# Opening of a two-layer fp32 kernel: the eight modulation weight units get memory of their own (that of the rounded weights), TensorE takes two of their products, GpSimd none, VectorE six, and the first unit starts on half of the features

## Chip, cores and metric

The kernel runs on one core of a Trainium2 chip. The metric is the device time of one execution in microseconds (us), as the median of three executions; beside it stands one profiled execution, from which all rows are read.

## The reference, cut to what matters

Two transformer-like blocks follow each other on 256 tokens of 1024 features. The change touches only the beginning of the first one:

```
c_act = silu(c)                                   # 1024 values
mod   = c_act @ w_mod + b_mod                     # 1024 x 3072; shift, scale, gate
h     = rms_norm(x, g_norm) * (1 + scale) + shift
proj  = h @ w_in                                  # 1024 x 8192, the first big product
```

`shift` and `scale` need two thirds of `w_mod`: 1024 rows of 2048 numbers, 8 MB. Everything after `proj` (a gated linear recurrence, dilated attention, output products, and then the second block with four feed-forward networks) depends on `h`.

## The kernel before, in words

All weights of the program lie in device memory as a row of "units" of 128 partitions x 2048 fp32 (1 MB each). SyncE's queue (SP) loads them in order into `raw`, a ring of four slots (`RING`). Each unit u that is a matmul weight is split in two: ScalarE writes its rounded part `whi` (`hi()`, L380) and VectorE the rest `wlo = raw - whi` (`lo()`, L1096); TensorE multiplies each with `feed_hi` and `feed_lo`, the two parts of the activations, in three passes (L1860 to L1862). One unit is 12 matmuls of 512 columns for each of the two token tiles t = 0, 1. A group is four units; TensorE does all four for t = 0, then for t = 1.

The first eight units, r = 0 to 7, are the modulation weights: unit r holds 128 rows of `w_mod`, one row on each partition. The sum over rows is made in two steps: an engine multiplies the unit by the column `c_act[:, r]` (one number for each partition), and TensorE then adds up the partitions by 16 matmuls with one column of ones (L1983, result in `aux`). Before the change GpSimd makes the products of r = 0 and 3 (`MOD_POOL`, L1033), VectorE adds up those of the other six in `mod_part` (L1246, the last one in two halves, L1251). The units use the same four slots of `raw` as all others, so the load of unit r + 4 waits until the product of unit r has been made (`wait_mod`), and the first matmul units u = 0 to 3 wait for those of r = 4 to 7.

Every engine has a program of its own, written out in order; semaphores tie them together. VectorE's order in the opening is: the sine and cosine tables (L1205 to L1233), the normalized rows `xn` (L1238), its modulation products, `lo(2)` for units 0 and 1, the sum of `aux` parts into `mod` and `scale_g` (L1256 to L1262), then for each token tile eight times `full = turn * scale_g + mod` (L1270, a chunk of 128 features each, from the transposed rows in `turn`), twice `feed_lo = full - feed_hi` (L1282), and `lo()` for the next unit. ScalarE makes `hi` of units 0 to 2, then `feed_hi` (L454) in halves of four chunks. TensorE waits at its first unit until both halves of `feed_lo` are there:

```
if g == 0:
    pe.wait_ge(first_fed, 2 * t + 2)
```

Its transposes of the rows of t = 1 stand ahead of that unit in its program. The second four of them need the second half of `turn` free, which is so when the last of the eight L1270 has run.

Of the kernel before, what the change touches and what calls it, by code (L numbers as in the profile page):

```python
# [70 lines left out]


# [8 lines left out]
MOD_POOL = (0, 3)  # L81
# [24 lines left out]
def build(nc, io):  # L106
    with ExitStack() as ctx:
# [8 lines left out]
        def sb(name, shape, dtype=F32):  # L116
# [8 lines left out]
        wlo = sb("wlo", [P, RING, UNIT], F32R)  # L125
        h = sb("h", [P, TOK, D])
# [62 lines left out]
        mod_pool = [placed("mod_pool0", [P, 2 * D], F32, base[0]),  # L189
                    placed("mod_pool1", [P, 2 * D], F32, base[0] - 4 * HEADS * SEQ)]  # L190
# [85 lines left out]
        setup_loaded = sem("setup_loaded")  # L276
        x_loaded = sem("x_loaded")
# [10 lines left out]
        mod_pooled = sem("mod_pooled")  # L288
# [58 lines left out]
        def mod_count(r):  # L347

            return sum((k in MOD_POOL) == (r in MOD_POOL) for k in range(r + 1))

        def wait_mod(engine, r):
            engine.wait_ge(mod_pooled if r in MOD_POOL else mod_used, mod_count(r))

# [12 lines left out]
        def _(act):  # L366
            n = {"u": 0, "e": [0, 0], "first": 0, "used": 0, "tb": 0, "ss": 0, "h": 0, "ple": 0, "mix": 0, "pre": 0}

            def hi(times=1, it=None):

                for _ in range(times):
# [5 lines left out]
                    act.wait_ge(loaded[u % RING], more * 16 + 16 * (raw_of(u) // RING + 1))  # L377
                    if u >= RING:
                        act.wait_ge(unit_used, more * RING + (u - RING + 1))
# [556 lines left out]
        def _(sp):  # L936
            sp.dma_start(cols[:, :], io["cols"]).then_inc(setup_loaded, 16)
            sp.dma_start(pos_i[:, :], io["pos_cols"]).then_inc(setup_loaded, 16)
            sp.dma_start(invf[:, :], io["invf"].partition_broadcast(P)).then_inc(setup_loaded, 16)
            sp.dma_start(h[:, :, :], io["x"].rearrange("(t p) d -> p t d", p=P)).then_inc(x_loaded, 16)  # L940
            sp.dma_start(ident[:, :], io["ident"]).then_inc(x_loaded, 16)
            for r in range(N_MOD1):
                if r >= RING:
                    wait_mod(sp, r - RING)
                sp.dma_start(raw[:, r % RING, :], io["units"][r]).then_inc(loaded[r % RING], 16)
            for j in range(RING):
                wait_mod(sp, N_MOD1 - RING + j)
                sp.dma_start(raw[:, j, :], io["units"][N_MOD1 + j]).then_inc(loaded[j], 16)
# [34 lines left out]
        def _(pool):  # L983
# [91 lines left out]
        def _(dve):  # L1075
# [118 lines left out]
            mark(dve.memset(mod_part[:, :], 0.0))  # L1194
            dve.wait_ge(setup_loaded, 16 * 3)
# [8 lines left out]

            mark(dve.tensor_copy(pos_f[:, :], pos_i[:, :]))  # L1205
# [35 lines left out]
            for r in range(N_MOD1):  # L1241
                if r in MOD_POOL:
                    continue
                dve.wait_ge(loaded[r % RING], 16 * (r // RING + 1))
                if r < N_MOD1 - 1:
                    dve.scalar_tensor_tensor(mod_part[:, :], raw[:, r % RING, :], c_act[:, r:r + 1], mod_part[:, :],  # L1246
                                             ALU.mult, ALU.add).then_inc(mod_used, 1)
# [1251 lines left out]
```

## Time and profile before

| what | value |
|---|---|
| median of three executions | 1509.49 us (1508.46 to 1510.73) |
| profiled execution, its own time | 1509.22 us |
| its span, first to last instruction | 1507.4 us |
| TensorE busy | 1435.8 us, 95% |
| VectorE busy | 886.2 us, 59% |
| ScalarE busy | 709.0 us, 47% |
| GpSimd busy | 100.8 us, 7% |
| loads | 272.52 MB, mean 181 GB/s |

The profiled execution's time is 1.8 us over its span (what lies around the span) and 0.3 us under the median. The opening is the stretch from 0 to about 53 us, where the first big matmul starts.

### The profile page before, as it was taken

Reading aid. Unit: us, or ns where it says so; the run is one execution under the profiler, and the core shown is the slowest. Engines: PE = TensorE matmul, PEld = TensorE weight load, DVE = VectorE, ACT = ScalarE, POOL = GpSimd, SP = SyncE. Lnnn points to the kernel's source line nnn. Section 1 sums busy time; section 2 is a strip of 40 time slices with the busy share of each in tenths; the row PEclk is TensorE's granted clock in tenths of the full one; section 3 lists DMA queues with packets and bytes.
Section 4 is the critical chain, followed back from the end, with each engine's and each line's share of the span. In section 5 each row is a group of like instructions: output and inputs, shape, how many; then the busy total and the mean of one; then the engine's idle time right before and its main releaser. Section 6 shows DMA issues by size and latency. Waiting matters only on the chain.

```text
span 1507.4 us, 17138 instructions
## 1 busy us (share of the span) xinstructions
PE 1435.8 (95%) x6622; PEld 1184.3 (79%) x6622; DVE 886.2 (59%) x818; ACT 709.0 (47%) x701; POOL 100.8 (7%) x95
## 2 busy tenths in 40 slices
PE   4899899899999999999999999999999999999997
PEld 4788777677888877788888877888888877888886
DVE  8856575976555465656545375554676354744535
ACT  2446756445454355745434354453544453543433
POOL 3000100002000020011000010000101110200001
PEclk9999999999999999999999999999999999999999
DMA  6754433574645544336445465645455454645541
GB/s 258 305 204 178 156 114 112 192 278 160 223 171 194 195 166 155 113 138 209 155 179 198 164 227 192 223 161 201 164 199 194 149 178 150 227 150 194 184 179 42
DMA packets 40510, 272.52 MB, mean 181 GB/s; under 512 B 4866, under 2 KB 5890, under 8 KB 8835
## 3 DMA queue, kind: packets, MB, share of 16 engines
q1 hardware_dynamic: 36992, 261.65, 48.0%
q10 hardware_dynamic: 3458, 10.04, 1.9%
q8 instruction: 43, 0.70, 0.2%
q14 instruction: 17, 0.13, 0.0%
HBM read 270.62 MB, written 1.05 MB: 180 GB/s over the span
## 4 chain that ended last, share of the span: by engine, by line
PE 83%; DVE 11%; ACT 3%; issue 2%; DMA 1%; POOL 0%; DVEq 0%; SPq 0%; POOLq 0%; ACTq 0%
PE acc L1860 25%; PE acc L1862 25%; PE acc L1861 25%; PE turn L1913 3%; DVE wlo L1096 3%; ACT whi L380 1%; DMA raw<-in_units 1%; DVE gate_part L1484 1%; PE aux L2164 1%; DVE xn L1150 1%; DVE h L1166 1%; DVE red L1227 1%; DVE feed_lo L1134 0%; PE turn L2014 0%; PE aux L2320 0%
## 5 line engine op out<-in xcount | busy, mean ns | idle before, releaser
L1096 DVE TENSOR_TENSOR wlo<-raw,whi 128x2048 fp32r<-128x2048 f32 x233 | 533.4, 2300 | 276.7 <-ACT whi L380 276.6
L1860 PE MATMUL acc<-whi,feed_hi 128*128 128x512 f32 (+1 forms) x1504 | 601.0, 400 | 11.7 <-DVE feed_lo L1134 7.8
L1862 PE MATMUL acc<-whi,feed_lo 128*128 128x512 f32 (+1 forms) x1504 | 588.6, 391 | 0.0
L1861 PE MATMUL acc<-wlo,feed_hi 128*128 128x512 f32 (+1 forms) x1504 | 587.8, 391 | 0.0
L380 ACT ACTIVATE whi<-raw 128x2048 fp32r<-128x2048 f32 x233 | 445.6, 1916 | 291.9 <-PE acc L1862 264.4
L1860 PEld LDWEIGHTS acc<-whi,feed_hi 128*128 128x128 f32 x1504 | 285.1, 190 | 71.3 <-issue 10.5
L1862 PEld LDWEIGHTS acc<-whi,feed_lo 128*128 128x128 f32 x1504 | 284.9, 189 | 60.7
L1861 PEld LDWEIGHTS acc<-wlo,feed_hi 128*128 128x128 f32 x1504 | 285.5, 190 | 56.8 <-issue 1.2
L1860 PE MATMUL acc<-whi,hid_hi 128*128 128x512 f32 x352 | 138.0, 392 | 0.0
L1862 PE MATMUL acc<-whi,hid_lo 128*128 128x512 f32 x352 | 137.1, 389 | 0.0
L1861 PE MATMUL acc<-wlo,hid_hi 128*128 128x512 f32 x352 | 137.0, 389 | 0.0
L1862 PEld LDWEIGHTS acc<-whi,hid_lo 128*128 128x128 f32 x352 | 66.1, 188 | 13.8
L1861 PEld LDWEIGHTS acc<-wlo,hid_hi 128*128 128x128 f32 x352 | 66.1, 188 | 13.3
L1860 PEld LDWEIGHTS acc<-whi,hid_hi 128*128 128x128 f32 x352 | 66.1, 188 | 13.3
L608 ACT ACTIVATE hid_hi<-turn 128x512 f32 (+2 forms) x48 | 26.4, 550 | 99.2 <-PE turn L1913 99.2
L1513 DVE TENSOR_TENSOR hid_lo<-turn,hid_hi 128x512 f32 (+2 forms) x48 | 30.8, 642 | 71.7 <-ACT hid_hi L608 71.7
L997 POOL TENSOR_SCALAR ms<-ss 128x1 f32<-128x1 f32 x20 | 14.7, 733 | 863.8 <-ACT xn L400 823.8
L1913 PE MATMUL turn<-ident,xn 128*128 128x128 f32 x250 | 36.4, 286 | 32.6 <-DVE xn L1238 20.5
L1913 PEld LDWEIGHTS turn<-ident,xn 128*128 128x128 f32 x250 | 30.3, 147 | 38.8 <-issue 23.6
L1504 DVE SCALAR_TENSOR_TENSOR hid<-acc,pre_rs,sgl 128x512 f32<-128x512 f32 (+1 forms) x48 | 33.8, 704 | 44.9 <-ACT sgl L601 41.0
L1134 DVE TENSOR_TENSOR feed_lo<-turn,feed_hi 128x512 fp32r<-128x512 f32 x48 | 31.0, 685 | 35.1 <-ACT feed_hi L422 35.1
L422 ACT ACTIVATE feed_hi<-turn 128x512 fp32r<-128x512 f32 x48 | 26.1, 592 | 49.3 <-PE turn L1913 49.0
(312 smaller groups left out, 898.7 us busy)
## 6 DMA issues: line engine op xcount, KB each, us to landing
raw<-in_units SPq DMA_DIRECT2D x245, 1024.0 KB, 4.9
gpost<-in_norm_g ACTq DMA_DIRECT2D x8, 512.0 KB, 5.0
gpre<-in_norm_g ACTq DMA_DIRECT2D x6, 512.0 KB, 6.3
h<-in_x SPq DMA_DIRECT2D x1, 1024.0 KB, 5.9
w_ax<-in_w_ax SPq DMA_DIRECT2D x1, 1024.0 KB, 9.4
bgate<-in_b_gate SPq DMA_DIRECT2D x1, 1024.0 KB, 12.0
out<-h SPq DMA_DIRECT2D x2, 512.0 KB, 2.6
decay<-in_decay ACTq DMA_DIRECT2D x1, 768.0 KB, 4.5
```

Source lines behind the costliest of these rows:

```text
L380: act.activation(whi[:, u % RING, :], raw[:, u % RING, :], ACT.Copy).then_inc(hi_ready, 1)
L422: act.activation(dst[:, 4 * i:4 * i + 4, lanes(t)], turn[:, b, :].rearrange("p (c s) -> p c s", c=4), ACT.Copy).then_inc(fed_hi, 1)
L608: act.activation(dst, turn[:, b, 0:P * count].rearrange("p (c s) -> p c s", c=count), ACT.Copy).then_inc(fed_hi, 1)
L1096: dve.tensor_tensor(wlo[:, u % RING, :], raw[:, u % RING, :], whi[:, u % RING, :].bitcast(F32), ALU.subtract).then_inc(lo_ready, 1)
L1134: dve.tensor_tensor(dst[part], turn[:, b, :].rearrange("p (c s) -> p c s", c=4), hi_part[part].bitcast(F32), ALU.subtract).then_inc(moved[ ...
L1150: dve.tensor_tensor(xn[:, t, halves[half]], h[:, t, halves[half]], gpre[:, halves[half]], ALU.mult)\
L1504: dve.scalar_tensor_tensor(hid[:, t, 0:tiles, :], up, pre_rs[:, t:t + 1], sgl[:, t, 0:tiles, :], ALU.mult, ALU.mult)\
L1513: dve.tensor_tensor(hid_lo[:, at, lanes(t)], turn[:, b, 0:P * count].rearrange("p (c s) -> p c s", c=count), hid_hi[:, at, lanes(t)].bitca ...
L1860: pe.matmul(out, xh, wh, start=first, stop=False)
L1861: pe.matmul(out, xh, wl, start=False, stop=False)
L1862: return pe.matmul(out, xl, wh, start=False, stop=last)
L1913: last = pe.transpose(turn[:, b, P * i:P * i + P], part, ident[:, :])
```

## The change

What it does: `mod_raw`, 8 units of room, is laid over `whi` and `wlo` (4 + 4 slots), which nothing uses before unit 0. Modulation unit r lands in it, each with a semaphore of its own, and the first four matmul units land in `raw`; none of these twelve loads waits. Instead, ScalarE waits before it writes `whi[u]` (that is where unit r = u lay) until the product of r = u is made; `wlo[j]` lies over unit r = 4 + j, which VectorE itself has read. TensorE makes the products of r = 0 and 1 itself: 16 matmuls each with the unit as weights and `c_act[:, r]` as the moving column. GpSimd has none. VectorE makes r = 2 to 7, the first as a plain product, so the clearing of `mod_part` goes. VectorE adds TensorE's two parts and the bias before `lo(2)`, and the third after it. The small loads of positions, `invf` and `ident` go from SP's queue to the start of ScalarE's queue, and the waits are split (`cols`, the two table inputs, `x`, `ident`). The work of a token tile on VectorE is interleaved, and TensorE's unit 0 waits for the first half of `feed_lo` alone, unit 1 for the second.

```
+        mod_raw = placed("mod_raw", [P, N_MOD1, UNIT], F32, base[0] - 8 * RING * UNIT)
...
         def wait_mod(engine, r):
-            engine.wait_ge(mod_pooled if r in MOD_POOL else mod_used, mod_count(r))
+            if r in MOD_PE:
+                engine.wait_ge(mod_columns, MOD_PE.index(r) + 1)
+            else:
+                engine.wait_ge(mod_used, mod_count(r))
...  ScalarE, hi()
-                    if u >= RING:
+                    if u < RING:
+                        wait_mod(act, u)
+                    else:
                         act.wait_ge(unit_used, more * RING + (u - RING + 1))
...  ScalarE, start
-            act.wait_ge(setup_loaded, 16 * 3)
+            act.dma_start(pos_i[:, :], io["pos_cols"]).then_inc(setup_loaded, 16)
+            act.dma_start(invf[:, :], io["invf"].partition_broadcast(P)).then_inc(setup_loaded, 16)
+            act.dma_start(ident[:, :], io["ident"]).then_inc(ident_loaded, 16)
+            act.wait_ge(cols_loaded, 16)
             act.activation(c_act[:, :], cols[:, COL["c"]:COL["c"] + KC], ACT.Silu).then_inc(c_ready, 1)
-            act.wait_ge(x_loaded, 16 * 2)
+            act.wait_ge(x_loaded, 16)
...  SyncE
-            sp.dma_start(cols[:, :], io["cols"]).then_inc(setup_loaded, 16)
-            sp.dma_start(pos_i[:, :], io["pos_cols"]).then_inc(setup_loaded, 16)
-            sp.dma_start(invf[:, :], io["invf"].partition_broadcast(P)).then_inc(setup_loaded, 16)
+            sp.dma_start(cols[:, :], io["cols"]).then_inc(cols_loaded, 16)
             sp.dma_start(h[:, :, :], io["x"].rearrange("(t p) d -> p t d", p=P)).then_inc(x_loaded, 16)
-            sp.dma_start(ident[:, :], io["ident"]).then_inc(x_loaded, 16)
             for r in range(N_MOD1):
-                if r >= RING:
-                    wait_mod(sp, r - RING)
-                sp.dma_start(raw[:, r % RING, :], io["units"][r]).then_inc(loaded[r % RING], 16)
+                sp.dma_start(mod_raw[:, r, :], io["units"][r]).then_inc(mod_loaded[r], 16)
             for j in range(RING):
-                wait_mod(sp, N_MOD1 - RING + j)
                 sp.dma_start(raw[:, j, :], io["units"][N_MOD1 + j]).then_inc(loaded[j], 16)
...  GpSimd
-            pool.wait_ge(c_ready, 1)
-            for r, product in zip(MOD_POOL, mod_pool):
-                pool.wait_ge(loaded[r % RING], 16 * (r // RING + 1))
-                pool.tensor_scalar(product[:, :], raw[:, r % RING, :], c_act[:, r:r + 1], None, ALU.mult)\
-                    .then_inc(mod_pooled, 1)
...  VectorE
-            mark(dve.memset(mod_part[:, :], 0.0))
-            dve.wait_ge(setup_loaded, 16 * 3)
+            dve.wait_ge(cols_loaded, 16)
...
+            dve.wait_ge(setup_loaded, 16 * 2)
             mark(dve.tensor_copy(pos_f[:, :], pos_i[:, :]))
...
+            dve.wait_ge(mod_columns, len(MOD_PE))
             mark(dve.tensor_tensor(mod[:, :], aux[:, 0, 0:2 * KC], cols[:, COL["b_mod"]:COL["b_mod"] + 2 * KC], ALU.add))
             settle()
+            mark(dve.tensor_tensor(mod[:, :], aux[:, 0, 2 * KC:4 * KC], mod[:, :], ALU.add))
+            settle()
+            dve.wait_ge(mods_ready, 1)
+            dve.wait_ge(mod_used, mod_count(N_MOD1 - 1))
+            lo(2)
+
+            dve.wait_ge(mod_summed, 1)
+            mark(dve.tensor_tensor(mod[:, :], aux[:, 1, 0:2 * KC], mod[:, :], ALU.add))
...
             for t in range(TOK):
+                modulated(t, next_turn(), 0, range(4))
+                b = next_turn()
+                modulated(t, b, 1, range(2))
+                first_rest(t, 0)
+                modulated(t, b, 1, range(2, 4))
+                first_rest(t, 1)
                 lo()
...  TensorE
+            for i, r in enumerate(MOD_PE):
+                pe.wait_ge(mod_loaded[r], 16)
                 for f in range(2 * KC):
                     at = 2 * KC * i + f
-                    last = pe.matmul(aux[:, 0, at:at + 1], part[:, P * f:P * f + P], ones[:, 0:1],
+                    last = pe.matmul(aux[:, 0, at:at + 1], mod_raw[:, r, P * f:P * f + P], c_act[:, r:r + 1],
                                      start=True, stop=True)
+                last.then_inc(mod_columns, 1)
+                if i == 0:
+                    feed_rows(xn[:, 0, :], staged_dve, "dve")
...
-                    if g == 0:
-                        pe.wait_ge(first_fed, 2 * t + 2)
+                if g == 0 and i < 2:
+                    pe.wait_ge(first_fed, 2 * t + i + 1)
```

`modulated(t, b, i, part)` is the old loop over L1270 for some of the chunks of half i, and `first_rest(t, i)` the old L1282 with its wait for `feed_hi`.

SyncE's queue, from the start of the program. Before:

```order
1 L937 DMA cols<-in_cols 128x104
2 L938 DMA pos_i<-in_pos_cols 128x4
3 L939 DMA invf<-in_invf 128x176
4 L940 DMA h<-in_x 128x2x1024
5 L941 DMA ident<-in_ident 128x128
6 L945 DMA raw<-in_units 128x2048 x4
7 L945 DMA raw<-in_units 128x2048 [waits mod_pooled]
8 L945 DMA raw<-in_units 128x2048 [waits mod_used] x2
9 L945 DMA raw<-in_units 128x2048 [waits mod_pooled]
10 L948 DMA raw<-in_units 128x2048 [waits mod_used] x4
11 L949 DMA w_ax<-in_w_ax 128x2048
```

and of the change:

```order
1 L951 DMA cols<-in_cols 128x104
2 L952 DMA h<-in_x 128x2x1024
3 L954 DMA mod_raw<-in_units 128x2048 x8
4 L956 DMA raw<-in_units 128x2048 x4
5 L957 DMA w_ax<-in_w_ax 128x2048
6 L958 DMA bias_124<-in_bias 128x384
```

Eight waits are gone from between the loads, and three small loads have left this queue.

VectorE, from the end of `lo(2)` (the two `wlo`) to the first `lo()` behind it. Before:

```order
30 L1096 TENSOR_TENSOR wlo<-raw,whi 128x2048 [waits hi_ready] x2
31 L1256 TENSOR_TENSOR mod<-aux,cols 128x16 [waits mod_summed]
32 L1260 TENSOR_TENSOR mod<-aux,mod 128x16 [waits dve_step] x2
33 L1262 SCALAR_TENSOR_TENSOR scale_g<-mod,cols 128x8 [waits dve_step]
34 L1270 TENSOR_SCALAR full<-turn,scale_g,mod 128x128 [waits turned0,dve_step]
35 L1270 TENSOR_SCALAR full<-turn,scale_g,mod 128x128 x2
36 L1270 TENSOR_SCALAR full<-turn,scale_g,mod 128x128 [waits dve_step]
37 L1270 TENSOR_SCALAR full<-turn,scale_g,mod 128x128 [waits turned1]
38 L1270 TENSOR_SCALAR full<-turn,scale_g,mod 128x128 x2
39 L1270 TENSOR_SCALAR full<-turn,scale_g,mod 128x128 [waits dve_step]
40 L1282 TENSOR_TENSOR feed_lo<-full,feed_hi 128x4x128 [waits fed_hi] x2
41 L1096 TENSOR_TENSOR wlo<-raw,whi 128x2048 [waits hi_ready]
```

and of the change:

```order
33 L1268 TENSOR_TENSOR mod<-aux,mod 128x16 [waits mod_summed]
34 L1270 SCALAR_TENSOR_TENSOR scale_g<-mod,cols 128x8 [waits dve_step]
35 L1277 TENSOR_SCALAR full<-turn,scale_g,mod 128x128 [waits turned0,dve_step]
36 L1277 TENSOR_SCALAR full<-turn,scale_g,mod 128x128 x2
37 L1277 TENSOR_SCALAR full<-turn,scale_g,mod 128x128 [waits dve_step]
38 L1277 TENSOR_SCALAR full<-turn,scale_g,mod 128x128 [waits turned1]
39 L1277 TENSOR_SCALAR full<-turn,scale_g,mod 128x128
40 L1290 TENSOR_TENSOR feed_lo<-full,feed_hi 128x4x128 [waits fed_hi]
41 L1277 TENSOR_SCALAR full<-turn,scale_g,mod 128x128
42 L1277 TENSOR_SCALAR full<-turn,scale_g,mod 128x128 [waits dve_step]
43 L1290 TENSOR_TENSOR feed_lo<-full,feed_hi 128x4x128 [waits fed_hi]
44 L1099 TENSOR_TENSOR wlo<-raw,whi 128x2048 [waits hi_ready]
```

Two small sums have moved ahead of the two `wlo`, and the first `feed_lo` stands between the sixth and the seventh chunk instead of behind the eighth. On TensorE, as it is now, the transposes of t = 1 still stand ahead of unit 0:

```order
10 L2004 MATMUL aux<-ones,mod_part 128x1 x7
11 L1929 MATMUL turn<-ident,xn 128x128 [waits moved0,staged_dve]
12 L1929 MATMUL turn<-ident,xn 128x128 x3
13 L1929 MATMUL turn<-ident,xn 128x128 [waits moved1]
14 L1929 MATMUL turn<-ident,xn 128x128 x3
15 L1876 MATMUL acc<-whi,feed_hi 128x512 [waits lo_ready,first_fed]
```

Here only the wait of the last row has changed its count; `moved1` is raised by the eighth chunk.

## Rows read from the trace of the kernel before

**Rows 1.** Busy time by stretch: stretch, length, PE, PEld, DVE, ACT, POOL, clock, DMA share, GB/s

```profile
60.00:120.00 60.00, 60.00 (x283) 49.94 (x282) 33.32 (x53) 27.71 (x21) 0.00 (x0) 1.00 0.47 171
```

**Rows 2.** Waits of TensorE, 0 to 110 us: total, times, longest

```profile
PE turn L1913 <- DVE xn L1238: 20.5, 1, 20.5
```

**Rows 3.** Timeline to 26 us (start, length, what); the first row is of the chain

```profile
1.65 4.79 DMA invf<-in_invf
...
9.17 1.65 DVE L1227 SCALAR_TENSOR_TENSOR red<-trn,red 128x352 f32<-128x352 f32 x3
...
12.54 5.04 DVE L1227 SCALAR_TENSOR_TENSOR red<-trn,red 128x352 f32<-128x352 f32 x3
13.48 5.46 POOL L1033 TENSOR_SCALAR mod_pool<-raw,c_act 128x2048 f32<-128x2048 f32 x1
...
17.62 1.51 DVE L1231 TENSOR_SCALAR red<-red 128x352 f32<-128x352 f32 x1
...
19.56 0.74 DVE L1238 TENSOR_SCALAR xn<-h,rs 128x1024 f32<-128x1024 f32 x1
...
19.75 5.86 POOL L1033 TENSOR_SCALAR mod_pool<-raw,c_act 128x2048 f32<-128x2048 f32 x1 [0.81 <-DMA raw<-in_units]
...
20.22 5.93 DVE L1238 TENSOR_SCALAR xn<-h,rs 128x1024 f32<-128x1024 f32 x1
```

**Rows 4.** Timeline, 33 to 48.3 us

```profile
33.39 2.35 DVE L1246 SCALAR_TENSOR_TENSOR mod_part<-raw,c_act,mod_part 128x2048 f32<-128x2048 f32 x1 [0.21 <-DMA raw<-in_units]
...
38.45 2.48 DVE L1251 SCALAR_TENSOR_TENSOR mod_part<-raw,c_act,mod_part 128x1024 f32<-128x1024 f32 x2
...
39.78 6.98 PE L1983 MATMUL aux<-ones,mod_part 128*128 128x1 f32 x32 [3.95 <-DVE mod_part L1251]
...
43.32 1.91 ACT L380 ACTIVATE whi<-raw 128x2048 fp32r<-128x2048 f32 x1 [0.56 <-DMA raw<-in_units]
45.26 2.29 DVE L1096 TENSOR_TENSOR wlo<-raw,whi 128x2048 fp32r<-128x2048 f32 x1 [0.18 <-ACT whi L380]
...
47.31 1.91 ACT L380 ACTIVATE whi<-raw 128x2048 fp32r<-128x2048 f32 x1 [2.08 <-DMA raw<-in_units]
...
48.09 0.17 DVE L1262 SCALAR_TENSOR_TENSOR scale_g<-mod,cols 128x8 f32<-128x8 f32 x1
```

**Rows 5.** Loads: the one issued at 3.10, then two of one stretch

```profile
raw<-in_units SPq DMA_DIRECT2D x1, 1024.0 KB, 9.2
...
L945 SPq DMA_DIRECT2D raw<-in_units x2: 635/672/710, 4.2 to 5.0; - x2
...
DMA to landing us min/median/max: 13.0/13.9/14.7
```

**Rows 6.** Timeline, 48.3 to 62 us

```profile
48.29 2.90 DVE L1270 TENSOR_SCALAR full<-turn,scale_g,mod 128x128 f32<-128x128 f32 x8
49.89 0.63 ACT L454 ACTIVATE feed_hi<-full 128x512 fp32r<-128x512 f32 x1 [0.66 <-DVE full L1270]
...
51.25 1.11 PE L1913 MATMUL turn<-ident,xn 128*128 128x128 f32 x4 [0.23 <-DVE full L1270]
...
51.95 0.69 DVE L1282 TENSOR_TENSOR feed_lo<-full,feed_hi 128x512 fp32r<-128x512 f32 x1 [0.16 <-ACT feed_hi L454]
52.56 2.29 DVE L1096 TENSOR_TENSOR wlo<-raw,whi 128x2048 fp32r<-128x2048 f32 x1
...
52.70 0.79 PE L1860 MATMUL acc<-whi,feed_hi 128*128 128x512 f32 x1 [0.33 <-DVE feed_lo L1282]
...
59.02 2.29 DVE L1096 TENSOR_TENSOR wlo<-raw,whi 128x2048 fp32r<-128x2048 f32 x1
...
61.91 0.39 PE L1860 MATMUL acc<-whi,feed_hi 128*128 128x512 f32 x1
```

**Rows 7.** Loads by line over the whole span: count, KB, median us to landing

```profile
gpre<-in_norm_g ACTq DMA_DIRECT2D x6, 512.0 KB, 6.3
...
ident<-in_ident SPq DMA_DIRECT2D x1, 64.0 KB, 7.2
```

More of the change, by code:

```diff
@@ L287, in build @@
         mod_used = sem("mod_used")
-        mod_pooled = sem("mod_pooled")
+        mod_loaded = [sem(f"mod_loaded{r}") for r in range(N_MOD1)]
+        mod_columns = sem("mod_columns")
         mods_ready = sem("mods_ready")
@@ L347, in mod_count @@
         def mod_count(r):
-            return sum((k in MOD_POOL) == (r in MOD_POOL) for k in range(r + 1))
+            return sum(k not in MOD_PE for k in range(r + 1))
         def wait_mod(engine, r):
-            engine.wait_ge(mod_pooled if r in MOD_POOL else mod_used, mod_count(r))
+            if r in MOD_PE:
+                engine.wait_ge(mod_columns, MOD_PE.index(r) + 1)
+            else:
+                engine.wait_ge(mod_used, mod_count(r))
         def chunks(ap, n=4):
@@ L376, in hi @@
                     more = 0 if it is None else it
-                    act.wait_ge(loaded[u % RING], more * 16 + 16 * (raw_of(u) // RING + 1))
-                    if u >= RING:
+                    act.wait_ge(loaded[u % RING], more * 16 + 16 * (loads_of(u) // RING + 1))
+                    if u < RING:
+                        wait_mod(act, u)
+                    else:
                         act.wait_ge(unit_used, more * RING + (u - RING + 1))
@@ L1240, in _ @@
             dve.wait_ge(c_ready, 1)
[L1241 to L1246, printed above, removed]
+            for r in range(len(MOD_PE), N_MOD1):
+                dve.wait_ge(mod_loaded[r], 16)
+                if r == len(MOD_PE):
+                    dve.tensor_scalar(mod_part[:, :], mod_raw[:, r, :], c_act[:, r:r + 1], None, ALU.mult)\
+                        .then_inc(mod_used, 1)
+                elif r < N_MOD1 - 1:
+                    dve.scalar_tensor_tensor(mod_part[:, :], mod_raw[:, r, :], c_act[:, r:r + 1], mod_part[:, :],
@@ L1257, in _ @@
             settle()
-            for i in range(len(MOD_POOL)):
-                at = 2 * KC * (i + 1)
-                mark(dve.tensor_tensor(mod[:, :], aux[:, 0, at:at + 2 * KC], mod[:, :], ALU.add))
-                settle()
             mark(dve.scalar_tensor_tensor(scale_g[:, :], mod[:, KC:2 * KC], 1.0,
@@ L1968, in group_deep @@
                         hooks[2]()
-            pe.wait_ge(x_loaded, 16 * 2)
-            feed_rows(xn[:, 0, :], staged_dve, "dve")
+            pe.wait_ge(ident_loaded, 16)
             pe.wait_ge(pads_ready, 1)
-            for i, part in enumerate(mod_pool + [mod_part]):
-                if part is not mod_part:
-                    pe.wait_ge(mod_pooled, i + 1)
+            pe.wait_ge(c_ready, 1)
+            for i, r in enumerate(MOD_PE):
+                pe.wait_ge(mod_loaded[r], 16)
                 for f in range(2 * KC):
-                    if part is mod_part and f == 0:
-                        pe.wait_ge(mods_ready, 1)
-                    if part is mod_part and f == KC:
-                        pe.wait_ge(mod_used, mod_count(N_MOD1 - 1))
                     at = 2 * KC * i + f
-                    last = pe.matmul(aux[:, 0, at:at + 1], part[:, P * f:P * f + P], ones[:, 0:1],
+                    last = pe.matmul(aux[:, 0, at:at + 1], mod_raw[:, r, P * f:P * f + P], c_act[:, r:r + 1],
                                      start=True, stop=True)
+                last.then_inc(mod_columns, 1)
+                if i == 0:
+                    feed_rows(xn[:, 0, :], staged_dve, "dve")
+            for f in range(2 * KC):
+                if f == 0:
+                    pe.wait_ge(mods_ready, 1)
+                if f == KC:
+                    pe.wait_ge(mod_used, mod_count(N_MOD1 - 1))
+                last = pe.matmul(aux[:, 1, f:f + 1], mod_part[:, P * f:P * f + P], ones[:, 0:1], start=True, stop=True)
             last.then_inc(mod_summed, 1)
```

52 lines of the change are left out of this document (27 added, 25 removed).

## Prediction

> **What bounds the kernel now.** I read the busy time by stretch first. Behind the opening TensorE is busy for 60.00 of 60 us [rows 1]; there the other engines only have to keep up. TensorE's longest wait is 20.5 us for the first normalized rows [rows 2], and its first big matmul starts at 52.70 [rows 6]. So the change can move one number, the start of that matmul; what it moves is moved for the whole program, as all later waits are relative to TensorE.
>
> The chain of waits up to 52.70, from its end: `feed_lo` (51.95 + 0.69) released the matmul; before it stand the eight L1270 from 48.29 [rows 6], `scale_g` at 48.09, ready at 48.26, and ahead of that the `wlo` of unit 1, which began at 45.26 behind ScalarE's `whi` at 43.32, which waited for the landing of unit 1 [rows 4]. TensorE's last pass over `mod_part` (39.78 + 6.98 = 46.76) was done earlier. Unit 1 landed late because each load waited for a ring slot, that is for products, and these were late because VectorE was. GpSimd's products ran 13.48 to 18.94 and 19.75 to 25.61. VectorE's three L1227 took 5.04 us beside the first of them and 1.65 without it, L1231 took 1.51 where I put 0.36 (an estimate: `xn`, nearly three times as long, takes 0.74), `xn` took 5.93 beside the second and 0.74 ahead of it [rows 3]. That is 3.4 + 1.15 + 5.2 = 9.7 us of VectorE's time lost beside GpSimd.
>
> **The loads.** Units r = 0, 2 and 3 were issued at 3.10, 4.2 and 5.0 and landed after 9.2, 13.0 and 14.7 us, at 12.3, 17.2 and 19.7 [rows 5]: 2.5 us each. r = 5 landed at 33.3 and unit 1, four later, at 43.3 [rows 4]: 2.5 again. Unit 2 then came at 47.3, 4.0 us later, a slip of 1.5 us. Now twelve loads stand in the queue without a wait. `h` is issued two places earlier, by 0.93 us at SP's pace; since the bytes of `invf` and `ident` still pass through the same engines, I take 0.5 us. So r = 3 lands at 19.2, r = 7 at 29.2, unit 0 at 31.7, unit 1 at 34.2, unit 2 at 36.7. Bounds: 1.5 us earlier (r = 0 is issued 1.45 us earlier) and 1.5 us later (one slip).
>
> **Path by the loads.** From unit 1's landing to `scale_g` ready it took 48.26 - 43.32 = 4.94 us [rows 4]. Two of the small sums, 0.2 us each, are now done before, so 4.54: 34.2 + 4.54 = 38.7. I call this moment M; before it was 48.26.
>
> **Path by the products.** VectorE's last product in two halves takes 2.48, its first half 1.28; r = 7 landed at 29.2, with 0.2 for the wait and 1.28 TensorE can start at 30.7. Its 32 rows take 6.98 [rows 4], 37.7; with 0.1 for the signal and 0.4 for the sum and `scale_g` M would be 38.2. This path loses by 0.5. TensorE is free for it: 6.98 for r = 0 from 11.8 gives 18.8, 1.9 for the transposes (L1913, eight of them; four took 1.11 [rows 6]) 20.7, r = 1 27.7. That cost is hidden by the wait for VectorE; the cover is 3.0 us.
>
> **Path by the tables.** `invf` landed at 1.65 + 4.79 = 6.44, and `xn` was ready at 26.15; less 9.7 that is 16.4, or landing + 10.0 [rows 3]. A plain product of 2048 is not in the trace; between 0.74 (half the size, [rows 3]) and 2.35 (the sum with product, [rows 4]) I take 1.35, since the same kind of instruction at half the size takes 0.74. Then four of 2.35, 1.28, TensorE's 6.98 and 0.7 for the waits and small sums: M = landing of `invf` + 29.7, so 36.2 at 6.44. It stays hidden as long as `invf` lands before 9.0. Clearing `mod_part` lay in the wait for the loads and is worth nothing.
>
> **From M to the matmul.** Before: 52.70 - 48.26 = 4.44. Now: four chunks of 0.36 (2.90 for eight) end at M + 1.5, ScalarE's `feed_hi` runs M + 1.6 to 2.3 [rows 6], VectorE does two chunks meanwhile, `feed_lo` M + 2.3 to 3.0, the last two chunks to M + 3.8. The half start would allow the matmul at M + 3.1. But TensorE's second four transposes stand ahead of it and wait for the eighth chunk, which is now behind `feed_lo`: they start at M + 3.85 and hold TensorE some 0.9 of their 1.11 us. So the first matmul starts at M + 4.8, 0.35 later than before. The edit that is named for a start on half of the features gives nothing by itself: by the order of rows it costs 0.35.
>
> It also delays VectorE. The second `feed_lo` now waits for `feed_hi` of the eighth chunk with nothing to do meanwhile: M + 3.9 to 4.55 on ScalarE, `feed_lo` to M + 5.3, against M + 4.4 before. `wlo` of unit 2 (2.29) ends at M + 7.5, and it is wanted at M + 11.3. Then t = 1, which took 59.02 - 52.56 = 6.46 from `wlo` to `wlo` [rows 6], takes the same 0.6 more: `wlo` of unit 3 starts at M + 12.35 and ends at M + 14.65. TensorE reaches unit 3 after 61.91 - 52.70 = 9.2 [rows 6], at M + 14.0. There it waits 0.65. Before, that unit was ready at 61.31 for 61.91. Behind it VectorE has slack and the rest follows TensorE.
>
> ScalarE makes `whi` of unit 2 before `feed_hi`: landing 36.7 + 1.91 = 38.6, wanted at M + 1.6 = 40.3; with the slip of 1.5 it is 40.1, just hidden.
>
> **Sum.** Matmul at 38.7 + 4.8 = 43.5 instead of 52.70, 9.2 earlier; less 0.65 at unit 3: 8.55 us. The profiled execution took 1509.22, which is 0.27 under the median: 1509.22 - 8.55 = 1500.7 us.
>
> **A rule that bears on it.** In the trace loads of ScalarE's queue land after 6.3 us in the middle (`gpre`), beside SP's units; `ident`, on SP's queue behind `h`, took 7.2 [rows 7]. Issued at about 1.2, `invf` would land at 7.5 by the first, before 9.0, and cost nothing; at 8.4 by the second, again nothing. The Trainium skill, "DMA: Bandwidth & Descriptors", section on queues, rings and completion order, says that each DMA engine goes round the queues that have work and changes only after a whole packet. By that rule `invf` would wait behind one packet of `h` or of a unit, not behind the whole stream; the sum would be the one above. The trace has no small load beside twelve waiting ones, so this stays a rival.
>
> **The rivals.**
> The loads come sooner (0.2): unit 1 at 32.7, r = 7 at 27.7. Then the products' path gives M = 36.7 and the loads' path 37.2; the matmul comes at 42.0, the saving is 10.05: 1499.2. For it: the stream starts earlier and is never interrupted. Against it: 2.5 us per unit was the same in both stretches.
>
> `invf` is late on ScalarE's queue (0.2): at 12 us M = 41.7, the saving 5.55, 1503.7. For it: it shares the engines with `h` and megabytes behind it from its first moment, where it had them nearly alone before. Against it: the 6.3 us of `gpre`.
>
> A slip in the stream hits unit 1 (0.08), as it hit unit 2: M = 40.2, 1502.2; with two slips 1503.7.
>
> Slower (0.03): ScalarE's queue is served only after SP's stream, so that `invf` lands behind the units. VectorE's chain is then the opening. It decides from a landing at 17.5 us on: M = 47.2, and with the 0.35 + 0.65 above the saving is nil. After ten units (26.7) it would be M = 56.4 and 1518.4. Against it: `gpre` lands in the middle of a stream of units.
>
> The change doesn't do what it says (0.02): `invf` at 14.5 to 17.5, or TensorE waiting elsewhere later for what it no longer waits for here, gives 1506.5 to 1509. Against it: TensorE's 60.00 of 60 us [rows 1] behind the opening.
>
> **How the numbers follow.** My forecast's own case has 0.47, with 1499.7 to 1501.8 for the bounds of the hand-over (0.35 and 0.65 both gone, or 1 us more if the first 36 matmuls, which stood 0.256 us apart [rows 6], stand 0.03 farther apart). The range reaches from the early case less its hand-over terms, 1498.0, to the late `invf` and slips, 1504.5. A measurement of this kernel tells about 0.2%, 3.0 us, from no change: faster takes the first four cases, 0.95; no change 0.02; slower 0.03.
>
> **What would show it.** Right: the first L1876 at 43.5, not 52.70; a wait of 0.4 to 0.9 us of TensorE for `wlo` at unit 3; its wait for `xn` down to nothing beyond 18.8, since r = 0 fills it; `whi` of unit 1 waiting for its load at about 34; VectorE's `xn` ready by 17.5. Wrong: `invf` later than 9 us, L1230 (the old L1227) still in the tables at 18, TensorE's products of r = 1 ending past 30.7, or the ten loads farther apart than 2.5 us.

## The result and the profile after

| | median | range |
|---|---|---|
| before | 1510.11 us (4 executions) | 1508.46 to 1512.11 |
| changed | 1500.46 us (4 executions) | 1498.02 to 1501.50 |

The ratio is 0.9932, 95% interval 0.9916 to 0.9949: 9.65 us faster by the medians, 7.7 to 12.7 by the interval. Predicted were 1500.7 us. The profiled execution of the changed kernel took 1498.02 us, with a span of 1496.0.

The timeline of the changed kernel's opening (start, length, engine, what; in brackets the idle time before it and what ended it):

```profile
10.12 1.64 DVE L1230 SCALAR_TENSOR_TENSOR red<-trn,red 128x352 f32<-128x352 f32 x3
...
11.31 6.98 PE L1994 MATMUL aux<-c_act,mod_raw 128*128 128x1 f32 x32 [11.31 <-DMA ident<-in_ident]
...
13.49 1.64 DVE L1230 SCALAR_TENSOR_TENSOR red<-trn,red 128x352 f32<-128x352 f32 x3
...
16.59 0.75 DVE L1241 TENSOR_SCALAR xn<-h,rs 128x1024 f32<-128x1024 f32 x1
...
17.25 1.28 DVE L1247 TENSOR_SCALAR mod_part<-mod_raw,c_act 128x2048 f32<-128x2048 f32 x1
...
28.59 2.48 DVE L1254 SCALAR_TENSOR_TENSOR mod_part<-mod_raw,c_act,mod_part 128x1024 f32<-128x1024 f32 x2
...
29.93 6.99 PE L2004 MATMUL aux<-ones,mod_part 128*128 128x1 f32 x32 [3.21 <-DVE mod_part L1254]
...
33.50 1.91 ACT L391 ACTIVATE whi<-raw 128x2048 fp32r<-128x2048 f32 x1 [0.58 <-DMA raw<-in_units]
...
37.21 1.91 ACT L391 ACTIVATE whi<-raw 128x2048 fp32r<-128x2048 f32 x1 [1.79 <-DMA raw<-in_units]
...
37.86 0.17 DVE L1270 SCALAR_TENSOR_TENSOR scale_g<-mod,cols 128x8 f32<-128x8 f32 x1
...
40.31 0.69 DVE L1290 TENSOR_TENSOR feed_lo<-full,feed_hi 128x512 fp32r<-128x512 f32 x1
...
41.83 1.11 PE L1929 MATMUL turn<-ident,xn 128*128 128x128 f32 x4 [1.04 <-DVE full L1277]
...
42.53 0.69 DVE L1290 TENSOR_TENSOR feed_lo<-full,feed_hi 128x512 fp32r<-128x512 f32 x1 [0.76 <-ACT feed_hi L468]
42.59 0.77 PE L1876 MATMUL acc<-whi,feed_hi 128*128 128x512 f32 x1
...
50.41 2.28 DVE L1099 TENSOR_TENSOR wlo<-raw,whi 128x2048 fp32r<-128x2048 f32 x1
```

Both series of three L1230 take 1.64 us, and the second `xn` 0.75, where [rows 3] had 5.04 and 5.93. The load of unit 1 lands at 33.50 and not at 43.32 [rows 4]; `scale_g` is ready at M = 38.03, the first big matmul starts at 42.59. The same stretch shows the two things that were forecast against the change: the first half of `feed_lo` is ready at 41.00, but the transposes ahead of the matmul wait 1.04 us for the eighth chunk, and the second `feed_lo` stands behind 0.76 us of idle time.

The waits of TensorE from 40 us on (engine, line, waited for: total, times, longest), and the chain where it comes to unit 3:

```profile
PE turn L1929 <- DVE full L1277: 3.8, 2, 2.8
PE acc L1876 <- DVE wlo L1099: 0.2, 1, 0.2
...
50.50 2.21 DVE wlo L1099
52.75 0.50 PE acc L1876
```

Here M is, as in the prediction, the moment when `scale_g` is ready. `wlo` of unit 3 ends at 52.69, M + 14.66, and TensorE starts unit 3 at 52.75. Before it was 61.91 [rows 6]. Up to here the change has brought 9.16 us between these two profiles. The span is 11.4 us shorter; the other 2.2 lie behind unit 3, where a second profile of the changed kernel (below) does not show them.

Why the wait is 0.2 and not the forecast 0.65 is seen in the starts of the first matmuls of unit 0:

```profile
45.30 0.63 PE L1876 MATMUL acc<-whi,feed_hi 128*128 128x512 f32 x1
45.73 0.52 PE L1877 MATMUL acc<-wlo,feed_hi 128*128 128x512 f32 x1
46.08 0.39 PE L1878 MATMUL acc<-whi,feed_lo 128*128 128x512 f32 x1
46.31 0.39 PE L1876 MATMUL acc<-whi,feed_hi 128*128 128x512 f32 x1
```

They start 0.43 us apart up to 45.73, and 0.23 apart from 46.08 on. 512 columns in 0.43 us are 1.2 GHz; the shorter step fits the 2.4 GHz level better than the lower one (my inference from the steps: the granted-clock column reads 1.00 for the whole opening all the same). The kernel before:

```profile
54.14 0.63 PE L1860 MATMUL acc<-whi,feed_hi 128*128 128x512 f32 x1
54.57 0.47 PE L1861 MATMUL acc<-wlo,feed_hi 128*128 128x512 f32 x1
54.87 0.40 PE L1862 MATMUL acc<-whi,feed_lo 128*128 128x512 f32 x1
55.11 0.39 PE L1860 MATMUL acc<-whi,feed_hi 128*128 128x512 f32 x1
```

It had the short step from 54.87 on, 2.2 us after its first matmul; here that came 3.5 us after. So TensorE came to unit 3 later by 0.6 us and found `wlo` nearly ready. I call the time from the first matmul to the first short step the slow stretch.

This bears on the 9.16 too. Before the change TensorE did not wait at unit 3 (`wlo` was ready at 61.31), so 61.91 moves with the slow stretch. With one of 3.5 us it would have been some 62.5, and the change would have brought some 9.8 (an estimate from these rows).

### The profile page after: what moved, and what is told of

It reads as the page before. It is cut to its first block, busy times and chain, and to the rows that moved or that the text cites. A ratio compares the mean times of both kernels' runs of the same rounds, so it can differ in the third digit from the quotient of the medians.

```text
span 1496.0 us, 17141 instructions
## 1 busy us (share of the span) xinstructions
PE 1433.3 (96%) x6622; PEld 1182.6 (79%) x6622; DVE 873.4 (58%) x817; ACT 709.1 (47%) x701; POOL 89.9 (6%) x93
## 3 DMA queue, kind: packets, MB, share of 16 engines
HBM read 270.62 MB, written 1.05 MB: 182 GB/s over the span
## 4 chain that ended last, share of the span: by engine, by line
PE 82%; DVE 10%; ACT 3%; issue 2%; DMA 2%; SPq 0%; POOL 0%; DVEq 0%; POOLq 0%; ACTq 0%
PE acc L1876 25%; PE acc L1878 25%; PE acc L1877 25%; PE turn L1929 3%; DVE wlo L1099 3%; DMA raw<-in_units 2%; ACT whi L391 1%; DVE gate_part L1500 1%; PE aux L2184 1%; DVE xn L1153 1%; DVE h L1169 1%; DVE feed_lo L1137 0%; PE turn L2034 0%; PE aux L2340 0%; PE aux L2215 0%
## 5 line engine op out<-in xcount | busy, mean ns | idle before, releaser
L1876 PE MATMUL acc<-whi,feed_hi 128*128 128x512 f32 (+1 forms) x1504 | 600.3, 399 | 11.4 <-DVE feed_lo L1137 7.9
L1878 PEld LDWEIGHTS acc<-whi,hid_lo 128*128 128x128 f32 x352 | 66.1, 188 | 13.8
L1929 PE MATMUL turn<-ident,xn 128*128 128x128 f32 x250 | 37.4, 291 | 12.2 <-DVE xn L1153 8.3
```

What stands on the lines that cost most here:

```text
L1876: pe.matmul(out, xh, wh, start=first, stop=False)
L1878: return pe.matmul(out, xl, wh, start=False, stop=last)
L1929: last = pe.transpose(turn[:, b, P * i:P * i + P], part, ident[:, :])
```

## The experiments

"Unit 3" is the start of its first matmul at t = 0, the 37th big matmul (idle-time ones not counted); whatever waits in the opening lies ahead of it. A line that begins with "..." has all edits of the lines above it, from "transposes behind unit 0" on. All are read from one profiled execution each.

| kernel | M | first matmul | unit 3 | span less unit 3 | granted clock |
|---|---|---|---|---|---|
| before | 48.26 | 52.70 | 61.91 | 1445.5 | 0.990 |
| changed | 38.03 | 42.59 | 52.75 | 1443.3 | 0.992 |
| changed, again | 38.11 | 42.68 | 52.84 | 1445.1 | 0.989 |
| memory alone | 46.99 | 51.42 | 61.67 | 1447.5 | 0.988 |
| loads wait | 46.30 | 50.88 | 61.05 | 1444.9 | 0.989 |
| small loads on SP | 38.82 | 43.39 | 53.55 | 1444.7 | 0.989 |
| `invf` late | 47.57 | 52.14 | 62.71 | 1444.4 | 0.990 |
| whole features | 38.12 | 42.55 | 52.49 | 1443.4 | 0.992 |
| transposes behind unit 0 | 37.75 | 40.78 | 52.48 | 1442.4 | 0.994 |
| ... and `wlo` of unit 3 ahead | 38.05 | 41.09 | 51.93 | 1443.4 | 0.992 |
| ... and `wlo` of unit 1 behind | 37.32 | 40.57 | 50.91 | 1443.1 | 0.992 |
| ... and idle-time matmuls | 37.16 | 40.50 | 50.54 | 1442.1 | 0.992 |
| ... and more of them | 38.79 | 41.82 | 51.89 | 1446.8 | 0.989 |
| the line but one, `whi` of unit 2 behind | 38.06 | 41.09 | 51.17 | 1442.3 | 0.992 |

The fifth column holds only work that none of these kernels changes. It scatters by 5.4 us, mostly with the granted clock, and that scatter is what the medians have to be read against. A straight line through the 100 executions of all these kernels gives 1.07 us less for 0.001 more of granted clock. With that taken out (an estimate, as it puts executions on four chips together) the changed kernel is 10.4 us under the one before, give or take 0.7.

**The changed kernel again.** No edit.

> The changed kernel once more, as the control of this set. First big matmul at 42.6 (within 0.6), wlo of unit 3 ready at M + 14.7, where M is the end of scale_g; 9 to 10 us under the kernel before. It also tells how much of the opening differs from run to run: the first twelve matmuls took 3.77 us before and 4.40 in the changed kernel's profile. If that is the run, it varies here; if it is the order of work, it is 4.4 again.

1500.34 us, ratio 0.9931 (0.9910 to 0.9952). M, first matmul and unit 3 agree with the first profile within 0.1 us. The slow stretch was 2.2 us instead of 3.5, and TensorE waited 0.8 us for `wlo` at unit 3 instead of 0.2; unit 3 began at the same moment. So VectorE sets that moment, and the length of the slow stretch is the run's. So are nearly all of the 2.2 us behind unit 3: here the rest is 1445.1, beside 1445.5 before.

**Memory alone.** The kernel before with `mod_raw` and its waits, and nothing else of the change.

```
+        mod_raw = placed("mod_raw", [P, N_MOD1, UNIT], F32, base[0] - 8 * RING * UNIT)
...
-                if r >= RING:
-                    wait_mod(sp, r - RING)
-                sp.dma_start(raw[:, r % RING, :], io["units"][r]).then_inc(loaded[r % RING], 16)
+                sp.dma_start(mod_raw[:, r, :], io["units"][r]).then_inc(mod_loaded[r], 16)
```

> The kernel before with mod_raw alone: the twelve loads wait for nothing, but GpSimd keeps its two products, VectorE its six, and the small loads and the order of features are the old ones. My theory: each half of the change alone is worth little, since VectorE beside GpSimd is nearly as late as the loads were. xn at 26, five sums of 2.36 to 38.0, half of the last to 39.3, TensorE to 46.3, M = 47.1, first matmul 51.5: 1.2 us under the kernel before. Rival: the loads were the bound and VectorE only followed; then M is near 39 and most of the 9 us are here.

1508.25 us, ratio 0.9976 (0.9964 to 0.9987). In its timeline the loads are early and VectorE is late:

```profile
20.06 5.93 DVE L1239 TENSOR_SCALAR xn<-h,rs 128x1024 f32<-128x1024 f32 x1
...
25.91 11.88 DVE L1247 SCALAR_TENSOR_TENSOR mod_part<-mod_raw,c_act,mod_part 128x2048 f32<-128x2048 f32 x5
...
34.42 1.91 ACT L384 ACTIVATE whi<-raw 128x2048 fp32r<-128x2048 f32 x1 [0.58 <-DMA raw<-in_units]
...
46.82 0.17 DVE L1265 SCALAR_TENSOR_TENSOR scale_g<-mod,cols 128x8 f32<-128x8 f32 x1
```

`xn` still takes 5.93 us beside GpSimd's product, then five sums follow without a wait, and M is 46.99 (47.1 expected) though unit 1 landed 9 us sooner. The rival, that the loads were the bound and VectorE followed, is out.

**Loads wait.** The changed kernel with the old waits between the loads.

```
             for r in range(N_MOD1):
+                if r >= RING:
+                    wait_mod(sp, r - RING)
                 sp.dma_start(mod_raw[:, r, :], io["units"][r]).then_inc(mod_loaded[r], 16)
             for j in range(RING):
+                wait_mod(sp, N_MOD1 - RING + j)
```

> The changed kernel, but each load waits as before until the product of the unit four places earlier is made. My theory: r = 4 waits for TensorE's first product (18.4), r = 5 for its second (26.9), so r = 5 lands at 31.8, r = 7 at 36.7, unit 1 at 41.6, M = 46.1, first matmul 50.7, 2 us under the kernel before. Rival: the products' new split is what brings it; then M is under 41.

1507.70 us, ratio 0.9975 (0.9964 to 0.9987). VectorE is ready and waits for the load that waited for TensorE's second product:

```profile
17.42 1.28 DVE L1250 TENSOR_SCALAR mod_part<-mod_raw,c_act 128x2048 f32<-128x2048 f32 x1
...
31.91 4.83 DVE L1253 SCALAR_TENSOR_TENSOR mod_part<-mod_raw,c_act,mod_part 128x2048 f32<-128x2048 f32 x2 [6.23 <-DMA mod_raw<-in_units]
```

M is 46.30 (46.1 expected). Each half alone moves M by 1.3 and 2.0 us, both by 10.2: two limits of nearly one length. Unit 3 moved by 0.2 and 0.9 only, since the run with memory alone had a slow stretch of 4.4 us. The medians of both runs are 3.2 and 3.8 us under the kernel before (2.0 to 5.4 by the intervals), more than the first matmul moved (1.3 and 1.8). With the granted clock taken out by the line above it is 1.8 and 2.7, each give or take 0.6. So part of the excess is the clock of those executions; what is left of it, 0.5 and 0.9, is not explained.

**Small loads on SP.** `pos_i`, `invf` and `ident` again on SyncE's queue in their old places.

> The changed kernel with the three small loads back on SyncE's queue in their old places. My theory: the move did little; invf lands at 6.4 instead of 7.8, which is hidden (the tables' path has 1 to 2 us to spare), and the units come 0.5 to 0.9 us later, since h is issued 0.93 later: unit 1 lands at 34.0 to 34.5, M = 38.5 to 39.0, unit 3 starts at 53.3 to 53.7 instead of 52.8. Rival: the three loads cost the units the same on either queue; then unit 1 lands at 33.5 again.

```profile
13.96 0.74 DVE L1241 TENSOR_SCALAR xn<-h,rs 128x1024 f32<-128x1024 f32 x1
...
16.98 1.29 DVE L1247 TENSOR_SCALAR mod_part<-mod_raw,c_act 128x2048 f32<-128x2048 f32 x1 [1.61 <-DMA mod_raw<-in_units]
...
34.30 1.91 ACT L391 ACTIVATE whi<-raw 128x2048 fp32r<-128x2048 f32 x1 [0.58 <-DMA raw<-in_units]
```

The tables are done 2.0 us sooner, and VectorE then waits for the loads; unit 1 lands at 34.30, 0.8 later than in the changed kernel, and M and unit 3 are 0.8 later. The move to ScalarE's queue is worth 0.8 us, as `h` and the units start two places earlier. The one execution took 1500.14 us, which says nothing at this size.

**`invf` late.** On SyncE's queue behind the first four modulation units.

```
                 sp.dma_start(mod_raw[:, r, :], io["units"][r]).then_inc(mod_loaded[r], 16)
+                if r == 3:
+                    sp.dma_start(invf[:, :], io["invf"].partition_broadcast(P)).then_inc(setup_loaded, 16)
```

> The changed kernel with the load of invf put on SyncE's queue behind the first four modulation units, so that it lands at about 19 us instead of 7.8. It is the slow rival of the prediction made on purpose. My theory: the tables' path takes over by its formula, M = landing of invf + 29.7, so M = 48 to 49 and the first matmul at 53, not earlier than in the kernel before. Rival: VectorE has slack there (it waited 0.1 us per product for the loads), so M is under 45.

It landed 14.7 us after its issue at 3.8, at 18.5, and `xn` was ready at 28.1. M was 47.57 where the formula gives 48.2: 0.4 of the difference lies in the tables and `xn`, 9.6 us behind the landing and not 10.0. The first matmul came at 52.14 (53 expected), unit 3 at 62.71, 0.8 later than before the change, with a slow stretch of 4.8 us; 1508.94 us in one execution. So the slow rival was a real mechanism, and its price was right to 0.6 us; what did not happen is its condition.

**Whole features.** The old order on VectorE, and TensorE waits for both halves.

```
                 modulated(t, next_turn(), 0, range(4))
-                b = next_turn()
-                modulated(t, b, 1, range(2))
+                modulated(t, next_turn(), 1, range(4))
                 first_rest(t, 0)
-                modulated(t, b, 1, range(2, 4))
                 first_rest(t, 1)
...  TensorE
-                if g == 0 and i < 2:
-                    pe.wait_ge(first_fed, 2 * t + i + 1)
+                if g == 0 and i == 0:
+                    pe.wait_ge(first_fed, 2 * t + 2)
```

> The changed kernel with the old order of features: all eight chunks, then both feed_lo, and TensorE's unit 0 waits for both halves. My theory: the half start costs by itself. First matmul at M + 4.45 (it was M + 4.56 in the changed kernel), wlo of unit 3 ready at M + 13.1 instead of M + 14.7, so TensorE doesn't wait there and starts unit 3 0.4 to 1.1 us earlier than the changed kernel's 52.8. Rival, the edit's own claim: the half start brings something; then the first matmul is later than M + 4.8 here.

First matmul at M + 4.43, `wlo` of unit 3 at 48.87 + 2.29 = 51.16, M + 13.04, and no wait there. Unit 3 starts at 52.49, 0.3 earlier than in the changed kernel, less than the 0.4 to 1.1 expected: the slow stretch was a long one here (3.6 us), and TensorE itself was the limit. The half start costs 0.3 us with a slow stretch like this; with one as short as in the changed kernel's second run it would be some 0.9 (an estimate: the wait there, 0.8, and the 0.1 of the first matmul). The one execution took 1497.95 us.

**Transposes behind unit 0.**

```
-            feed_rows(xn[:, 1, :], staged_dve, "dve")
+            n["dve"] += 1
+            pe.wait_ge(staged_dve, n["dve"])
+            turns(chunks(xn[:, 1, 0:BANK]))
...
+                if s == 0:
+                    turns(chunks(xn[:, 1, BANK:D]))
```

> The changed kernel with TensorE's second four transposes behind unit 0, VectorE as it is. My theory: they are what holds the half start back, so the first matmul comes at M + 3.1 (41.1); but wlo of unit 3 is still ready at M + 14.7, so unit 3 starts at 52.7 to 52.8 as before and TensorE waits there for 0.8 us and more: nothing gained. Rival: the opening ends with the first matmul; then unit 3 starts at 51.9, as in the run with wlo of unit 3 ahead.

The waits of TensorE, 40 to 75 us:

```profile
PE acc L1876 <- DVE wlo L1099: 0.5, 1, 0.5
PE acc L1876 <- DVE feed_lo L1290: 0.3, 1, 0.3
```

The first matmul comes at M + 3.03. Unit 3 starts at 52.48, M + 14.73, as in the changed kernel (M + 14.72 and 14.73): all of the 1.5 us is given back in unit 0's slow matmuls, in the transposes behind it and in the wait for `wlo`. The one execution took 1496.71 us, 3.6 to 3.8 under the changed kernel's medians; its granted clock was the highest of all, 0.994, and unit 3 stood where it stood before, so this is no gain of the edit.

**And `wlo` of unit 3 ahead of the features of t = 1.**

```
                 first_rest(t, 1)
-                lo()
+                if t == 0:
+                    lo(2)
```

> The changed kernel with TensorE's second four transposes of t = 1 behind unit 0, and on VectorE wlo of unit 3 ahead of the features of t = 1. My theory: the first matmul starts at M + 3.1 (41.1 with M = 38.0) instead of M + 4.6, and TensorE doesn't wait at unit 3, so unit 3 starts 1.7 to 2.0 us earlier than in the changed kernel, and the time is 1.7 us less than its. Rival: the features of t = 1, now later by 2.3 us, become the wait (at unit 0 of t = 1) and take it back; then TensorE waits there for feed_lo.

1498.84 us, ratio 0.9922 (0.9895 to 0.9949). No wait at unit 3, nor at t = 1; unit 3 at M + 13.88, 0.8 to 0.9 earlier, half of what I expected. In this run and the one before it ten and eleven of unit 0's twelve matmuls were slow (7 and 4 in the two profiles of the changed kernel): the earlier start is spent on slow matmuls.

**And `wlo` of unit 1 behind the features of t = 0.** `lo(1)` ahead of the sum, `lo(3)` behind the first features.

> The kernel of unit 0 early and wlo of unit 3 ahead, and also wlo of unit 1 behind the features of t = 0 instead of ahead of the sum of the modulation. My theory: M then goes by the products' path, TensorE's last pass ends at 36.9, M = 37.45 instead of 38.03; first matmul at M + 3.1 = 40.55; wlo of units 1, 2, 3 are ready at M + 7.5, 9.8, 12.1, each just ahead of TensorE, so unit 3 starts at 51.3 and the time is 0.6 us under the one with 51.93. Rival: wlo of unit 1 comes too late for unit 1 and TensorE waits there; then unit 3 starts no earlier than 51.9.

1496.59 us, ratio 0.9917 (0.9890 to 0.9943). M = 37.32, 0.13 from the forecast of the products' path; unit 3 at 50.91, earlier than the 51.3 expected. TensorE did not wait for `wlo` of unit 1.

**And idle-time matmuls ahead of unit 0.** Their result is used by nothing.

```
+            def spin(times):
+                for _ in range(times):
+                    pe.matmul(acc[1][:, 0:BANK], whi[:, 0, 0:P], whi[:, 0, 0:BANK], start=True, stop=True)
+
+            pe.wait_ge(hi_ready, 1)
+            spin(4)
...
             turns(chunks(xn[:, 1, 0:BANK]))
+            spin(1)
```

> The kernel with wlo of unit 1 behind the features, and five matmuls of 512 columns whose result nothing uses, in TensorE's idle time ahead of unit 0 (four ahead of the transposes of t = 1, one behind them). It measures the slow start: in all runs so far the first 4 to 11 matmuls of unit 0 stood 0.43 apart and the others 0.23, wherever unit 0 began. My theory: it is the clock, 1.2 GHz until TensorE has been given wide matmuls for some time, so the idle-time ones take over part of the slow stretch: at most 4 slow ones are left in unit 0, unit 3 starts 0.6 to 1.4 us earlier than 50.9, and the time is that much less. Rival: the slow start belongs to unit 0 itself (its operands, PSUM), then 7 or more are slow again and the first matmul is 0.2 to 0.4 late besides.

1495.60 us, ratio 0.9911 (0.9887 to 0.9936). Its timeline on TensorE:

```profile
36.61 2.05 PE L2009 MATMUL acc<-whi 128*128 128x512 f32 x4
38.83 1.09 PE L1930 MATMUL turn<-ident,xn 128*128 128x128 f32 x4 [0.17 <-DVE full L1277]
39.57 0.64 PE L2009 MATMUL acc<-whi 128*128 128x512 f32 x1
40.50 0.50 PE L1877 MATMUL acc<-whi,feed_hi 128*128 128x512 f32 x1 [0.29 <-DVE feed_lo L1290]
40.84 0.39 PE L1878 MATMUL acc<-wlo,feed_hi 128*128 128x512 f32 x1
...
45.02 0.47 PE L1877 MATMUL acc<-whi,feed_hi 128*128 128x512 f32 x1 [1.05 <-DVE wlo L1099]
...
50.54 0.39 PE L1877 MATMUL acc<-whi,feed_hi 128*128 128x512 f32 x1
```

The idle-time matmuls are slow themselves (four in 2.05 us), and of unit 0 only the first step, 0.34 us, is longer than 0.23. The slow stretch is thus not tied to unit 0. TensorE is now so early that it waits 1.05 us for `wlo` of unit 1. So little is left of it at unit 3, 50.54 instead of 50.91: 0.4 us, where 0.6 to 1.4 were expected. That part of the expectation failed, as VectorE set the pace.

**More of them, in the last pass.** Eight ahead of TensorE's last pass, three inside it, and ScalarE's `whi` of unit 2 behind `feed_hi`.

> The kernel of the run before it, and: eight such matmuls in TensorE's wait for VectorE's last product (26.7 to 29.9), three inside its last pass, and on ScalarE whi of unit 2 behind feed_hi of t = 0 instead of ahead of it. ScalarE writes one extra tile for their operand. My theory: the last pass runs at 2.4 GHz, its 32 rows take 4 us instead of 6.98 plus 0.7 for the three, so the products' path ends at 34.6, M goes by wlo of unit 0 (35.35) and is 35.8, first matmul 38.9, unit 3 at 49, 1.5 to 2 us earlier than without. Rival: matmuls of one column let the clock fall in the middle of the pass, which then takes 6 us or more and M is 36.5 to 37.5; or the eight end past 29.9 and delay the pass.

1500.65 us, ratio 0.9934 (0.9915 to 0.9954): the theory fell.

```profile
26.71 3.76 PE L2004 MATMUL acc<-feed_hi 128*128 128x512 f32 x8
30.27 1.70 PE L2017 MATMUL aux<-ones,mod_part 128*128 128x1 f32 x8
31.84 0.77 PE L2004 MATMUL acc<-feed_hi 128*128 128x512 f32 x1
...
36.67 1.70 PE L2017 MATMUL aux<-ones,mod_part 128*128 128x1 f32 x8
38.23 2.05 PE L2021 MATMUL acc<-whi 128*128 128x512 f32 x4
```

Eight rows of the pass take 1.70 us from its first to its last quarter, as before, and all wide matmuls up to the first of unit 0 are slow. The three inside the pass and the eight, which end 0.2 us too late for its start, make the way from VectorE's half product to M longer by 1.3 us; with loads 0.3 us later M is 38.79, 1.6 us later than in the run before. Of unit 0 one matmul was slow, and unit 3 came at 51.89 where 49 was expected.

**Without those, `whi` of unit 2 behind `feed_hi`.**

```
-            hi(RING - 1)
+            hi(RING - 2)
...
                 if t:
-                    hi()
+                    hi(2)
```

> The kernel with five idle-time matmuls ahead of unit 0, and on ScalarE whi of unit 2 behind feed_hi of t = 0. There VectorE waited 0.43 us for feed_hi, which waited for whi of unit 2, and TensorE then waited 1.1 us for wlo of unit 1. My theory: the whole chain moves by 0.3 to 0.4: first feed_lo at M + 2.3, wlo of unit 1 ready at M + 7.4, unit 3 starts at 49.7 instead of 50.1, wait at unit 1 still 0.8 to 1.1. The time is 1495 to 1496, which a measurement can't tell from the run without this edit. Rival: wlo of unit 2, now with a later whi, becomes the wait and unit 3 starts after 50.1.

1496.36 us, ratio 0.9909 (0.9892 to 0.9927). First matmul at M + 3.03 instead of M + 3.34, unit 3 at M + 13.12 instead of M + 13.38: relative to M the forecast 0.3. In absolute time it is later, 51.17 and not the 49.7 expected, as the units landed 0.9 us later in this execution. TensorE did not wait for `wlo` of unit 1: five of unit 0's matmuls were slow here, with the same idle-time matmuls ahead. This kernel and the one with idle-time matmuls have the lowest medians of all; they can't be told apart, and their intervals overlap those of the changed kernel. With the granted clock taken out as above they are 13.7 and 13.8 us under the kernel before, give or take 0.8 and 0.9, beside 10.4 for the changed kernel.

## Why the prediction was right, point by point

**The limit.** That the opening alone counts, and that what it moves is moved for the whole program, held: unit 3 moved by 9.16 and 9.07 us in the two profiles, the medians by 9.65 and, beside the second profile, by 11.2 (1511.49 to 1500.34). That the medians moved more fits the short slow stretch in the profile before.

**The two causes.** 9.7 us of VectorE's time lost beside GpSimd: the tables and `xn` took 7.77 to 17.34, that is landing of `invf` + 9.6 against the forecast 10.0. Loads 2.5 us apart without a wait: unit 1 at 33.5, forecast 34.2. The run with memory alone and the one with waiting loads show that both are needed. The prediction had the paths side by side, from which this follows, but it did not say it.

**The paths.** The loads' path bound, at 38.03 against 38.7, and the products' path stood 0.65 behind it (the run with `wlo` of unit 1 behind shows it at 37.32 to 37.4), forecast 0.5. `invf` landed at 7.8 (issue at 1.17 + 6.6), where the prediction's two estimates were 7.5 and 8.4. That the path of the tables was hidden with it is right, but by little: at an M of 38.0 the formula leaves 0.5 us (38.03 - 29.7 - 7.8), and 1.1 with the 29.1 that the run with `invf` late gave (47.57 - 18.5).

**From M on.** First matmul at M + 4.56, forecast 4.8, before 4.44: the half start did cost, by 0.12 for 0.35. The transposes held TensorE 0.76 us (41.83 to 42.59), not 0.9, and started 0.05 earlier than forecast. `wlo` of unit 3 at M + 14.66, forecast 14.65. The wait of 0.65 was 0.2 in one execution and 0.8 in the other, because TensorE's own arrival varies with its slow stretch. The forecast took the 9.2 us of 36 matmuls over from one execution as if they were fixed. Since VectorE set the moment of unit 3 either way, the sum suffered little: 8.55 forecast, 9.16 and 9.07 in the profiles, and the difference is the loads' earlier landing (M 0.6 to 0.7 earlier than forecast). The other end of the sum, 61.91 before the change, was the one that the slow stretch moves.

**How near, and how much of it is luck.** 1500.7 was forecast and 1500.46 measured, but the nearness is partly luck. The saving was 8.55 for a measured 9.65, and the kernel before took 1510.11 at the median here, 0.9 more than the 1509.22 from which the forecast subtracted (one profiled execution, not the median). The two differences cancel to 0.24 us, in a measurement whose interval is 5 us wide.

**The rivals.** Loads that come sooner: half of it came (0.7 of 1.5 us). `invf` late, and slower by it: the mechanism and its price were shown by the run made for it (48.2 by formula, 47.57 measured); the condition did not come true. The slip of a load hit unit 2 again (37.21, 3.7 after unit 1) and was hidden, as worked out. `invf` beside the waiting loads took 6.6 us from issue to landing, and 6.9 in the second run; behind four of them in their own queue it took 14.7.

That GpSimd's products hold up VectorE's instructions is shown by place and size: the series takes 5.04 beside a product and 1.64 without one. The two half runs separate it from the loads. With early loads and GpSimd's products (memory alone) `xn` takes 5.93; with the old waits and without the products (loads wait) it takes 0.75. What inside the chip does it, no run here shows.

## What to carry to other kernels

Where two engines or queues are late by nearly the same amount, taking away one lateness brings little (here 1.3 or 2.0 us) and both together the whole (10.2); write every path to the common end as a sum, and price an edit by the second-longest of them. An edit that frees the first instruction of a stage early may bring nothing: the instructions ahead of it in the same queue can still hold it, and a later item of the stage (here the fourth unit) can be the next wait. Look at both before the edit. Such small terms are read from the place of an event in the trace, since the time of the whole kernel scatters by more.

## What the hardware showed that I had not expected

TensorE's first wide matmuls start 0.43 us apart for 2.1 to 4.9 us, in a different length from run to run (2.2 and 3.5 us with one kernel), and the granted-clock column shows nothing of it. It had been busy with one-column matmuls for 7 us, which ended some 6 us ahead, with short transposes between. Five wide ones ahead of unit 0 left at most one slow matmul in two executions (one of them with eleven more wide ones before) and five in another. With eight in a row (3.5 us), followed by one-column ones with single wide ones between, the wide ones were still slow 15 us later.

With some ten 1 MB loads waiting, SyncE needs 2.1 us to issue the next load instead of 0.4 (2.11 us for `w_ax`); no load of the opening was late by it.
